# Rounded transpositions for branch C's queries and keys, staged by a copy, in a two-layer hybrid decoder

## The reference

```python
h = rms_norm(x, g_mix[l])
parts = jnp.split(h @ w_in[l], IN_SPLITS, axis=-1)
# A: sliding window, 8 heads on 2 key heads; B: latent attention, 8 heads
# C: three groups of 8 heads with dilations 1, 4, 16; M: 4 heads over 256 memory tokens
for g, (win, dil) in enumerate(C_PATTERNS):
    qc = apply_rope(rms_norm(cq.reshape(B, S, C_HEADS, C_HD), c_qn[l, g]), cos_h, sin_h)
    kc = apply_rope(rms_norm(ck.reshape(B, S, C_HEADS, C_HD), c_kn[l, g]), cos_h, sin_h)
    o_g, lse_g = dilated_group(qc, kc, vc, win, dil)
y = jnp.einsum('bsnc,ncd->bsnd', o, w_branch[l])
x = x + jnp.einsum('bsnd,de->bse', gates * y, w_out[l])
u = rms_norm(x, g_mlp[l]) @ w_up[l]
x = x + jnp.square(jax.nn.relu(u)) @ w_down[l]
```

## Time and profile before

| | us |
|---|---|
| median of 3 runs | 1154.24 (1153.82 to 1154.36) |
| the profiled execution, its own time | 1153.84 |
| its span, first to last instruction | 1152.1 |
| PE busy | 1146.4 |
| DVE busy | 861.6 |
| ACT busy | 696.0 |
| POOL busy | 152.1 |

### The profile page before, as it was taken

How to read it: one execution, slowest core, us unless ns; L and a number is a source line. 1 busy time by engine, 2 the same in 40 slices (tenths; PEclk the granted TensorE clock), 3 DMA queues, 4 the chain that set the end, 5 groups by cost and what they waited for, 6 DMA issues and landing times.

```text
span 1152.1 us, 17675 instructions
## 1 busy us (share of the span) xinstructions
PE 1146.4 (100%) x6212; PEld 970.1 (84%) x6212; DVE 861.6 (75%) x1442; ACT 696.0 (60%) x1132; POOL 152.1 (13%) x159
## 2 busy tenths in 40 slices
PE   9999999999999999999999999999999999999998
PEld 7888888888888888888888988888888888888887
DVE  6878988887776775665766888888877676766555
ACT  6868886755554464544575689776655445545442
POOL 6214613200000000000010144312000000000000
PEclk9999999999999999999999999999999999999999
DMA  9574636455466656666657555455454665666663
GB/s 299 186 222 145 169 122 205 120 183 183 156 215 205 183 169 196 187 196 185 209 163 209 149 150 164 146 165 166 147 191 138 204 196 172 192 187 193 190 190 103
DMA packets 128022, 205.96 MB, mean 179 GB/s; under 512 B 9158, under 2 KB 50720, under 8 KB 127808
## 3 DMA queue, kind: packets, MB, share of 16 engines
q1 hardware_dynamic: 122432, 194.64, 55.0%
q10 hardware_dynamic: 4720, 8.92, 2.6%
q0 software_dynamic: 784, 1.28, 0.4%
HBM read 200.41 MB, written 2.10 MB: 176 GB/s over the span
## 4 chain that ended last, share of the span: by engine, by line
PE 99%; DVE 1%; DMA 0%; issue 0%; ACTq 0%; DVEq 0%
PE ps_d L1807 24%; PE ps_d L1809 24%; PE ps_d L1808 24%; PE ps_b L1798 10%; PE ps_b L1795 5%; PE ps_b L1873 3%; PE ps_b L1840 3%; PE ps_b L1882 2%; PE ps_b L1920 2%; PE ps_d L1920 1%; DMA early<-in_g_mix_dram 0%; PE ps_d L1873 0%; DVE w_lo L1468 0%; DVE sums L1527 0%; PE ps_d L1746 0%
## 5 line engine op out<-in xcount | busy, mean ns | idle before, releaser
L1242 ACT ACTIVATE w_hi<-raw 128x1024 fp32r<-128x1024 f32 (+5 forms) x376 | 390.0, 1040 | 351.3 <-PE ps_d L1809 261.8
L1468 DVE TENSOR_TENSOR w_lo<-raw,w_hi 128x1024 fp32r<-128x1024 f32 (+5 forms) x376 | 448.1, 1201 | 200.6 <-ACT w_hi L1242 197.1
L1807 PE MATMUL ps_d<-w_hi,h_both 128*128 128x512 f32 (+3 forms) x704 | 279.5, 397 | 0.0
L1809 PE MATMUL ps_d<-w_hi,h_both 128*128 128x512 f32 (+3 forms) x704 | 267.2, 380 | 0.0
L1808 PE MATMUL ps_d<-w_lo,h_both 128*128 128x512 f32 (+3 forms) x704 | 266.6, 379 | 0.0
L1807 PE MATMUL ps_d<-w_hi,r_both 128*128 128x512 f32 (+1 forms) x552 | 217.5, 394 | 0.2 <-DVE w_lo L1468 0.2
L1808 PE MATMUL ps_d<-w_lo,r_both 128*128 128x512 f32 (+1 forms) x552 | 213.9, 388 | 0.0
L1809 PE MATMUL ps_d<-w_hi,r_both 128*128 128x512 f32 (+1 forms) x552 | 213.9, 387 | 0.0
L1809 PEld LDWEIGHTS ps_d<-w_hi,h_both 128*128 128x128 f32 x704 | 132.2, 188 | 24.9
L1807 PEld LDWEIGHTS ps_d<-w_hi,h_both 128*128 128x128 f32 x704 | 132.4, 188 | 23.8 <-DVE h_both L1606 0.7
L1808 PEld LDWEIGHTS ps_d<-w_lo,h_both 128*128 128x128 f32 x704 | 132.7, 188 | 20.8
(11 more groups left out here) (201 smaller groups left out, 1156.9 us busy)
## 6 DMA issues: line engine op xcount, KB each, us to landing
raw<-in_w_in_dram SPq DMA_DIRECT2D x154, 512.0 KB, 4.2
raw<-in_w_up_dram SPq DMA_DIRECT2D x64, 512.0 KB, 3.7
raw<-in_w_down_dram SPq DMA_DIRECT2D x64, 512.0 KB, 3.7
raw<-in_w_branch_dram SPq DMA_DIRECT2D x32, 512.0 KB, 4.1
raw<-in_m_w_kv_dram SPq DMA_DIRECT2D x16, 512.0 KB, 4.6
raw<-in_w_out_dram SPq DMA_DIRECT2D x16, 512.0 KB, 3.7
early<-in_b_gate_dram ACTq DMA_DIRECT2D x16, 256.0 KB, 4.6
raw<-in_w_in_dram SPq DMA_DIRECT2D x8, 384.0 KB, 4.0
```

The source lines that it names most:

```text
L1242: nc.scalar.activation(unit_in(w_hi, u), unit_in(raw, u), ACT.Copy).then_inc(hi_split, 1)
L1468: nc.vector.tensor_tensor(unit_in(w_lo, u), unit_in(raw, u), unit_in(w_hi, u).bitcast(F32), ALU.subtract).then_inc(lo_split, 1)
L1807: nc.tensor.matmul(o, hi[:, a["c"], cut], wh, start=a["first"], stop=False)
L1809: last = nc.tensor.matmul(o, lo[:, a["c"], cut], wh, start=False, stop=a["last"])
```

## The change

The six query and key tiles of C are no longer turned from their home. Once a token is rotated, ACT issues one DMA that copies it (SBUF to SBUF, 128 partitions of 4 KB) into a tile `tok_r` of the rounded type, and the tensor engine turns it from there, with an identity of the same type, into PSUM seen as the same type. The copy waits for M's last `pv`, for the rotated token, and for the turns of the token staged before. In the plan it is an ACT item of 0.1 us, and the turns come at least 2.8 us after it. The home is still released by the turns.

`tok_r` lies on M's keys (30 S to 34 S of `early`). For that B's turned probabilities shrink from 16 slots to 12: the steps of the first token half, which have one block of 128 columns, share a slot in pairs. The wishes of M's heads now end at 12 instead of 16 beyond the axis, and B's heads run from there to 8 before the gates. The identity is written as float32r; all other transpositions read a float32 view of it.

```diff
-P_RING, PT_RING = {"C": 4, "": 4, "o": 4}, {"A": 12, "M": 2, "B": 16, "C": 4}
+P_RING, PT_RING = {"C": 4, "": 4, "o": 4}, {"A": 12, "M": 2, "B": 12, "C": 4}
...
-    def turns(tok, count_, width, dest, mode="plain", gain=None, l=0, order=None):
+    def turns(tok, count_, width, dest, mode="plain", gain=None, l=0, order=None, after=None):
         plain_turns[dest] = []
+        staged = None
+        if after is not None:
+            done, job = tok_ready_of[tok]
+            staged = item("stage", "ACT", 0.1, [done, after, *held["staged"]], order=axis[0], after=after, behind=held["staged"], home=homes[tok],
+                          ready=tok_ready_at[tok], k=count("stage"))
+            tok_ready_of[tok] = (staged, 2.8), job
+            held["staged"] = []
         for c in range(0, count_, 2):
...
+            if staged:
+                held["staged"].append(tok_turns[tok][-1])
...
-            pt_place, pt_half = divmod(len(own), 2) if halves else (len(own), 0)
+            pt_place, pt_half = divmod(len(own), 2) if halves or branch == "B" and not tt else (len(own), 0)
+            if branch == "B" and tt:
+                pt_place -= B_H // 2
...
-            if branch != "A" and len(own) >= PT_RING[branch]:
+            if branch in "MC" and len(own) >= PT_RING[branch]:
...
-        b_from = axis[0] + 16.0
+        b_from = axis[0] + 12.0
...
-        pt_free["B"] = steps[-1]["pv"]
+        pt_free["B"] = m_last = steps[-1]["pv"]
...
-                      C_H // 2, 2 * HD, ("qC%d" if part == 0 else "kC%d") % g)
+                      C_H // 2, 2 * HD, ("qC%d" if part == 0 else "kC%d") % g, after=m_last)
...
-        spread(heads_of(l, "B", B_H), b_from, gates_from)
+        spread(heads_of(l, "B", B_H), b_from, gates_from - 8.0)
...
+        early_at = -(-nc.sbuf_base // 32) * 32
         early = sb("early", [P, 38 * S])
+        tok_r = nc.alloc_sbuf_tensor_at("tok_r", [P, TT, NW], F32R, offset=early_at + 30 * S * 4)
...
-        ident = sb("ident", [P, P])
+        ident = sb("ident", [P, P], F32R)
+        one = ident[:].bitcast(F32)
...
-        free_of_a, free_of_m = early[:, 0:6 * S], early[:, 26 * S:34 * S]
+        free_of_a, free_of_m = early[:, 0:6 * S], early[:, 26 * S:30 * S]
...
+                elif it.kind == "stage":
+                    act.wait_ge(pv_done, a["after"].a["k"] + 1)
+                    act.wait_ge(tok_ready, a["ready"] + 1)
+                    for t in a["behind"]:
+                        turned(act, t)
+                    act.dma_start(tok_r[:].bitcast(F32), home_of(a["home"])).then_inc(tok_staged, 16)
...
-                        if a["ready"] is not None:
+                        if a.get("staged"):
+                            pe.wait_ge(tok_staged, 16 * (a["staged"].a["k"] + 1))
+                        elif a["ready"] is not None:
...
-                        last = nc.tensor.transpose(ps_b[0:wd, b, k * P:(k + 1) * P], v, ident[:])
+                        to = ps_b[0:wd, b, k * P:(k + 1) * P]
+                        if a.get("staged"):
+                            v = tok_r[:, tt, c * wd:(c + 1) * wd]
+                            last = nc.tensor.transpose(to.bitcast(F32R), v, ident[:])
+                        else:
+                            last = nc.tensor.transpose(to, v, one)
```

More of the change, by code:

```diff
@@ L200, in plan @@
          "v": 0, "ready": 0, "pv": 0, "osplit": 0, "rotated": 0, "move": 0, "up": 0, "msplit": 0, "pselect": 0,
-         "ring": 0, "scale": 0, "lent": 0, "side": 0}
+         "ring": 0, "scale": 0, "lent": 0, "stage": 0, "side": 0}
     axis = [0.0]
@@ L222, in plan @@
     unit_chunks = []
-    held = {"sq": [], "x": [], "xjobs": (), "early": [], "heads": []}
+    held = {"sq": [], "x": [], "xjobs": (), "early": [], "heads": [], "staged": []}
     class Job:
@@ L399, in turns @@
             turn(("tok", tok), [done], c, min(2, count_ - c), width, dest, mode, gain, l, order=order, home=homes[tok],
-                 ready=tok_ready_at.get(tok), scaled=scaled_at.get(tok))
+                 ready=tok_ready_at.get(tok), scaled=scaled_at.get(tok), staged=staged)
+            if staged:
+                held["staged"].append(tok_turns[tok][-1])
     def head_turns(tok, i, side, gain, l):
@@ L996, in hybrid_block @@
                         "C": [probT_c[:, i] for i in range(TT)] + [tok[:, 0, i * NW:(i + 1) * NW] for i in range(PT_RING["C"] - TT)]}
-        free_of_a, free_of_m = early[:, 0:6 * S], early[:, 26 * S:34 * S]
-        turned_probs["B"] = turned_probs["M"] + [w[:, i * S:(i + 1) * S] for w, n in ((free_of_a, 6), (free_of_m, 8)) for i in range(n)]
-        assert len(turned_probs["B"]) == PT_RING["B"] == TT * B_H
+        free_of_a, free_of_m = early[:, 0:6 * S], early[:, 26 * S:30 * S]
+        turned_probs["B"] = turned_probs["M"] + [w[:, i * S:(i + 1) * S] for w, n in ((free_of_a, 6), (free_of_m, 4)) for i in range(n)]
+        assert len(turned_probs["B"]) == PT_RING["B"] == 3 * B_H // 2
         plain = {"qA": q_a, "kA": k_a, "qM": q_m, "kM": k_m, "q": q_b, "k": k_b}
@@ L1027, in hybrid_block @@
         o_hi_split, o_split = sem("o_hi_split"), sem("o_split")
-        heads_out = sem("heads_out")
+        heads_out, tok_staged = sem("heads_out"), sem("tok_staged")
         side_scored = [sem("side_scored%d" % i) for i in range(TT)]
@@ L1139, in _ @@
             nc.gpsimd.memset(no_mask[:], 0.0).then_inc(seeded, 1)
-            nc.gpsimd.memset(ident[:], 0.0).then_inc(pool_chain, 1)
+            nc.gpsimd.memset(one, 0.0).then_inc(pool_chain, 1)
             nc.gpsimd.memset(power[:], -0.5)
@@ L1144, in _ @@
             pool.wait_ge(pool_chain, 2)
-            nc.gpsimd.affine_select(out=ident[:], in_=ident[:], compare_op=ALU.not_equal, fill=1.0, base=0,
+            nc.gpsimd.affine_select(out=ident[:], in_=one, compare_op=ALU.not_equal, fill=1.0, base=0,
                                     pattern=[[-1, P]], channel_multiplier=1).then_inc(ident_ready, 1)
@@ L1745, in idle_turns @@
                 for _ in range(n):
-                    nc.tensor.transpose(ps_d[:, 1, 0, 0:P], ident[:], ident[:])
+                    nc.tensor.transpose(ps_d[:, 1, 0, 0:P], one, one)
             pe.wait_ge(ident_ready, 1)
@@ L1760, in _ @@
                     pe.wait_ge(g_first_landed, 16)
-                    nc.tensor.transpose(ps_d[:, 1, 1, 0:DC], g_first, ident[0:DC, 0:DC]).then_inc(g_first_turned, 1)
+                    nc.tensor.transpose(ps_d[:, 1, 1, 0:DC], g_first, one[0:DC, 0:DC]).then_inc(g_first_turned, 1)
                 elif it.kind == "gains_turn":
@@ L1764, in _ @@
                     pe.wait_ge(g_rows_landed, 16 * ALL_LOADS)
-                    nc.tensor.transpose(ps_b[:, b, 0:n_rows], g_rows, ident[0:n_rows, 0:n_rows]).then_inc(bank_full[b], 1)
+                    nc.tensor.transpose(ps_b[:, b, 0:n_rows], g_rows, one[0:n_rows, 0:n_rows]).then_inc(bank_full[b], 1)
                 elif it.kind == "chunk":
@@ L1881, in _ @@
                         own = 2 * k if a["odd"] else k
-                        last = nc.tensor.transpose(ps_b[:, b, k * P:(k + 1) * P], prob_of(st)[:, own * P:(own + 1) * P], ident[:])
+                        last = nc.tensor.transpose(ps_b[:, b, k * P:(k + 1) * P], prob_of(st)[:, own * P:(own + 1) * P], one)
                     last.then_inc(bank_full[b], 1)
```

## The result

The changed kernel takes 1156.24 us, the median of 15 runs (1154.98 to 1159.12), against 1154.24, a difference of 2.0 us. So the change made the kernel slower, by little, where 3.0 us less was forecast. Its profiled execution is one of its longest, 1158.56 us with a span of 1156.8.

A forecast was written before the change was run, and what follows sets the result against it. The tensor engine's issued work was taken as the bound. Turns -3.5 us and copies +0.5 made -3.0: 1150.8 for the profiled execution, 1151.2 for the median against 1154.24, range 1149.6 to 1157.0.

The forecast's parts named there:

- What bounds the kernel: Tensor engine, busy 1146.4 of 1152.1 us: its issued work sets the end; other engines count only if they make it wait.
- The turns: C's 96 transpositions on the tensor engine: 82 steps each 0.043 us shorter, 3.5 us off; bounds 4.4 off to 0.8 on.
- so it is the stream: C's turns: the 0.110 us step is set by streaming the identity, not by the weight load of 0.056.
- The 0.067 put down for the stream: Step expected for a rounded turn: one pass of 0.053 us plus 0.013, above the load of 0.056.
- the less likely case: Rival on C's turns: no shorter step, nothing off, copies stay; 1154.7 us, up to 1158 with late copies; chance 0.26.
- The copies: Twelve copies on ACT's queue, landing in 3.5 us: 0.1 us missing for one token per layer, as much again added; 0.5 on.
- 5.03 us of room: Planned time from one token's last rotation to its turn, where the copy was taken to need 3.65 us.
- the 3 us that I had named as the sign of being wrong: Tensor engine's waits on the copies: the prediction is wrong if they pass 3 us.
- The order: Moved turns, M's and B's heads and packing of B's turned blocks: 0 us; first token's turn still moves to about 170.
- The late copy: Rival: copies land in 5.1 to 5.3 us, 6.8 us of waits less 3.5 gained, 1157.5 us; chance 0.20, half slower.
- the sum of chances for slower: Chance of a slower kernel: 0.10 from late copies plus 0.08 from no shorter step, 0.18.
- the landing of 5 us for all copies: Copies before C's turns: lateness decides from a landing of about 5 us; between 4 and 5 it only eats the gain.

The follow-up runs named there:

- the kernel with plain float32 copies: Changed kernel with its copies, order and waits kept, but the staged tile turned in plain float32; 1159.40 us, ratio 1.0046 to the kernel before.
- the kernel with both mends: Changed kernel with the moves of C's third values behind the third copy and turns planned at least 4.2 us behind their copy; 1152.90 us.
- the kernel with the longest waits: Changed kernel with the planner's 2.8 us behind a copy set to 0.2; 1189.80 us, ratio 1.0303 to the kernel before.

## Why the prediction was wrong

- **What bounds the kernel** held: the tensor engine's own work and its waits account for the whole difference.
- **The turns** failed in the step "so it is the stream": that a load takes 0.056 us. What the earlier trace rows show is by how much one transposition was delayed on an idle array (by 0.03 in three others, behind the waits of the kernel with plain float32 copies), not how often loads can follow each other. In a run they follow each other every 0.085 us. In plain float32 this hid behind a step of 0.109; with the shorter stream it sets the pace, and at the end of a run the chunk's weights wait for it too, which makes the last step 0.09 instead of 0.03 (its next product then comes 0.02 sooner). The 0.067 put down for the stream was not too low: it takes 0.061 at most. So the term came out at 2.0 us instead of 3.5, although the count (82 steps, 14 runs) was right. The Trainium skill (TensorE: Matmul & The Clock Gate, section LDWEIGHTS) puts the load of 128 columns at 107 ns; in the trace loads of rounded turns follow each other every 85, and the measurement decides. What I had worked out from that rule, that the load bounds a turn, was right; that nothing comes off was not. I had called it the less likely case because one exposed load looked shorter.
- **The copies** failed in the step that put all twelve at one landing time of 3.5 us and only missed 0.1. The median landing was nearly right, 3.7. But a wait is set by the worst copy: 5.1 and 5.7 us for the third one of a layer, after 1.6 us and more in which it could not be issued. I had counted what stands behind the copy on ACT's queue and not what stands ahead of it, and the four moves of C's values were in the profile before, on the same queue. The third token, for which I had written 5.03 us of room, is the one that waited. Instead of 0.5 us the waits came to 4.2 in the profiled execution, and to about 3.4 in the median by the kernel with both mends. That is past the 3 us that I had named as the sign of being wrong.
- **The order** held: no cost shows for the packing, for M's and B's wishes and for the first token, whose turn moved from 156 to 166.8 without anyone waiting.
- **The rivals.** The late copy was the case that came, with 4.2 us of waits instead of the 6.8 of that rival and with less gain to set against it, so it decided long before the landing of 5 us for all copies that I had named. It had 0.20, and the sum of chances for slower was 0.18. The measured time lies inside my range only because its upper end stood for late copies; the forecast itself had the wrong sign. Two errors that add up make the 5.0 us between forecast and result: by the trace 1.5 us on the turns and 3.7 on the waits (0.2 too much), by the times of the kernel with both mends some 2.0 and 2.9.

## What to carry to other kernels

A transfer put in place of a direct read costs by its latest landings, not by its median (here three late copies of twelve made the loss), and the first place to look is what stands ahead of it on the queue that issues it. If an engine writes the data anyway, let it write the second form itself: here that turned 2.0 us lost into 1.8 gained. And when a step has two overlapping parts, the hidden one must be timed in a run of its own kind before the visible one is shortened.

## What the runs showed of the hardware that I had not expected

- Turns with 128 columns of weights were delayed by only 0.03 to 0.056 us on an idle array, and yet rounded ones follow each other only every 0.085; with 64 columns that bound is gone and 0.061 is left. Rounded transpositions step by as little as 0.06, when their weights were loaded ahead, plain float32 ones by 0.109.
- A wait of the tensor engine can cost more than itself. Behind the 1.9 us wait of the profiled run of the changed kernel the clock fell to 1.2 GHz and took 1.6 us more (three of its 15 runs have a lower mean clock), and it fell six times in the kernel with the longest waits. The length of the wait alone doesn't decide: no fall came behind one of 2.2 us in the kernel with plain float32 copies, nor behind one of 2.3 in the kernel with the longest waits. That the wait brings the fall is my reading of their order in time; no run tested it by itself.
